# A two-layer decoder trunk on one core: an earlier pivot for the norms, squares folded group by group, and the tokens that the last layer doesn't need

## The reference

```python
def _layer_norm(x, g, b):
    mu = jnp.mean(xf, axis=-1, keepdims=True)
    var = jnp.mean(jnp.square(xf - mu), axis=-1, keepdims=True)
    y = (xf - mu) * lax.rsqrt(var + LN_EPS) * g.astype(jnp.float32) + b.astype(jnp.float32)
...
    for l in range(DEPTH):
        m = _mixer(h, ...)
        h = _layer_norm(ALPHA * h + m, ln1_g[l], ln1_b[l])
        f = _conv_ffn(h, w_up[l], conv_w[l], conv_b[l], w_down[l])
        h = _layer_norm(ALPHA * h + f, ln2_g[l], ln2_b[l])
    return h[:, N_META:, :]
```

## Time and profile before

| | before |
|---|---|
| median of 3 runs | 2676.42 us (2675.54 to 2681.03) |
| the profiled execution | 2678.43 us |
| its span, first to last instruction | 2676.6 us |
| mean granted TensorE clock | 0.974 |
| TensorE matmul busy | 2549.4 us, 95% |
| VectorE busy | 1775.6 us, 66% |
| ScalarE busy | 1368.8 us, 51% |

### The profile page before, as it was taken

The page is one execution under the profiler, slowest core; times in us unless marked ns, Lnnn a source line. Parts: engine busy times, 40 slices in busy tenths (PEclk is TensorE's granted clock), DMA queues, the critical chain, the costliest instruction groups (busy, mean ns, idle before and its releaser), DMA issues.

```text
span 2676.6 us, 55946 instructions
## 1 busy us (share of the span) xinstructions
PE 2549.4 (95%) x21738; PEld 2464.7 (92%) x21738; DVE 1775.6 (66%) x2782; ACT 1368.8 (51%) x2127; POOL 11.9 (0%) x19
## 2 busy tenths in 40 slices
PE   6999999889999999999979999998899999999997
PEld 5999788879999999999979997888899999999997
DVE  6887487676666666544488874877766666664445
ACT  5444365365555555433364444653666666553334
POOL 0000000000000000000000000000000000000000
PEclk7999999989999999999989999998899999999998
DMA  4433133345555555555444331333455555555553
GB/s 170 143 121 125 66 109 103 126 134 177 169 179 174 170 179 171 177 173 165 166 144 146 120 129 60 113 101 118 149 181 180 180 188 181 179 183 189 173 187 107
DMA packets 109733, 401.91 MB, mean 150 GB/s; under 512 B 12177, under 2 KB 12177, under 8 KB 109585
## 3 DMA queue, kind: packets, MB, share of 16 engines
q1 hardware_dynamic: 108432, 395.15, 44.9%
q0 software_dynamic: 1152, 4.63, 0.4%
HBM read 397.50 MB, written 2.23 MB: 149 GB/s over the span
## 4 chain that ended last, share of the span: by engine, by line
PE 89%; DVE 7%; ACT 2%; issue 1%; DMA 1%; SPq 0%; ACTq 0%; DVEq 0%
PE ps L426 22%; PE ps L427 22%; PE ps L428 22%; PE ps L525 4%; PE ps L527 4%; PE ps L526 4%; PE ps L675 3%; PE ps L491 1%; PE ps L662 1%; PE ps L641 1%; PE ps L608 1%; DVE h L1183 1%; PE ps L500 1%; PE ps L505 1%; DVE h L1162 1%
## 5 line engine op out<-in xcount | busy, mean ns | idle before, releaser
L786 ACT ACTIVATE w_hi<-raw 128x1024 fp32r<-128x1024 f32 x728 | 763.3, 1056 | 765.4 <-PE ps L428 656.7
L1107 DVE TENSOR_TENSOR w_lo<-raw,w_hi 128x1024 fp32r<-128x1024 f32 x528 | 638.9, 1224 | 543.9 <-ACT w_hi L786 543.8
L427 PE MATMUL ps<-x_lo,w_hi 128*128 128x272 f32 (+1 forms) x2944 | 841.3, 286 | 0.0
L428 PE MATMUL ps<-x_hi,w_hi 128*128 128x272 f32 (+1 forms) x2944 | 839.9, 285 | 0.0
L426 PE MATMUL ps<-x_hi,w_lo 128*128 128x272 f32 (+1 forms) x2816 | 805.5, 286 | 18.8 <-DVE x_lo L1191 18.4
L428 PEld LDWEIGHTS ps<-x_hi,w_hi 128*128 128x128 f32 x2944 | 555.5, 189 | 0.0
L427 PEld LDWEIGHTS ps<-x_lo,w_hi 128*128 128x128 f32 x2944 | 555.4, 189 | 0.0
L426 PEld LDWEIGHTS ps<-x_hi,w_lo 128*128 128x128 f32 x2816 | 531.2, 189 | 20.5 <-issue 18.0
L426 PE MATMUL ps<-g_hi,w_lo 128*128 128x272 f32 (+1 forms) x1408 | 403.7, 287 | 4.9 <-DVE w_lo L1107 2.5
L427 PE MATMUL ps<-g_lo,w_hi 128*128 128x272 f32 (+1 forms) x1408 | 403.0, 286 | 0.0
L428 PE MATMUL ps<-g_hi,w_hi 128*128 128x272 f32 (+1 forms) x1408 | 401.4, 285 | 0.0
(11 more groups left out here) (266 smaller groups left out, 3306.1 us busy)
## 6 DMA issues: line engine op xcount, KB each, us to landing
raw<-stream SPq DMA_DIRECT2D x744, 512.0 KB, 3.4
h<-x SPq DMA_DIRECT2D x4, 544.0 KB, 6.3
out<-h SPq DMA_DIRECT2D x4, 544.0 KB, 2.7
cst<-consts POOLq DMA_DIRECT2D x2, 724.0 KB, 6.5
wkv<-w_kv POOLq DMA_DIRECT2D x2, 512.0 KB, 7.9
b_st<-ssm_b POOLq DMA_DIRECT2D x2, 512.0 KB, 9.3
c_st<-ssm_c POOLq DMA_DIRECT2D x2, 512.0 KB, 11.3
par<-params SPq DMA_DIRECT2D x1, 562.0 KB, 12.1
```

The source lines that it names most:

```text
L427: pe.matmul(acc, w_hi[:, slot, kk, cols], lo, start=False, stop=False)
L428: mm = pe.matmul(acc, w_hi[:, slot, kk, cols], hi, start=False, stop=k == tiles - 1)
L786: act.activation(w_hi[:, slot, :, :], raw[:, slot, :, :], ACT.Copy).then_inc(hi_made, 1)
L1107: dve.tensor_tensor(w_low(phase, slot), raw[:, slot, :, :], w_hi[:, slot, :, :].bitcast(F32), ALU.subtract).then_inc(in_lo_made if phase = ...
```

## The change

The pivot is the mean of the first four tiles (two groups) instead of twelve: `sum_pivot` adds them, one matmul of ones follows group 2, and `take_pivot` copies it, scaled, into a tile of its own. `center_early` adds the pivot to the first six tiles in one instruction. From group 3 on the pivot is added to h before the group's product arrives (`before_out`, `before_down`), and the product on top. Each group is squared by ScalarE as it ends (`group_square`), folded by VectorE (`fold_squares`, now in five parts) and added into hsum (`sum_means`), so that TensorE sums hsum and the last group for the mean. In down, input times alpha is prepared in the phase (`before_down`), and `after_down` is one add.

In `layer_norm` on VectorE the first shift of four tiles moves behind the spread. After out, the first low part of up moves ahead of the residual of the last group, and three instead of two low parts lie in the scaling loop; after down one stays ahead of the shift, and again three instead of two lie in the loop. The order of scaling, x_lo and shifts in the loop changes.

On TensorE, out and down have bodies of eight groups and are no longer loops. g_hi and g_lo become halves of one tensor, and down of the last layer uses `wide_block`: w_hi with both in one matmul of 512 columns, w_lo with g_hi in one of 256; `after_down` adds both halves (two instructions). In the last layer the query tiles of the input projection (iq and fq, 12 of 30), late, gated, fox and out work on tokens 14 on; GpSimd zeroes the first 14 tokens of those tiles with two memsets, for which TensorE waits ahead of the S5 steps, and the residual of gated scales the first 14 columns with an instruction of its own.

```diff
 PHASES = {"in": (15, DT // KB, 1), "glu": (4, UT // KB, 4), "late": (2, DT // KB, 2), "gated": (8, UT // KB, 4),
-          "fox": (8, 1, 1), "out": (8, 1, 4), "up": (FT, DT // KB, 2), "down": (8, FT // KB, 4)}
+          "fox": (8, 1, 1), "out": (8, 1, 8), "up": (FT, DT // KB, 2), "down": (8, FT // KB, 8)}
...
-PIVOT = 3 * DT // 4
+PIVOT = 4
+EARLY = 6
...
+        def group_done(n, g):
+            return first_group((n - 1) // 2, "out" if n % 2 else "down") + g + 3
...
-                with pe.Fori(0, groups // body) as it:
+                with ExitStack() as loop:
+                    it = loop.enter_context(pe.Fori(0, groups // body)) if groups > body else 0
...
+            def wide_block(phase, slot, b, bank, tiles, both, ready, t0):
+                lo_w, n = w_low(phase, slot), NT - t0
+                for kk in range(KB):
+                    k = b * KB + kk
+                    if ready and k % 2 == 0:
+                        pe.wait_ge(*ready(k))
+                    hi_lo = both(k)[:, :, t0:NT]
+                    for j in range(2):
+                        cols = slice(j * P, j * P + P)
+                        pe.matmul(ps[:, bank + j, 0:2 * n].rearrange("p (h t) -> p h t", h=2), w_hi[:, slot, kk, cols], hi_lo,
+                                  start=k == 0, stop=False)
+                        mm = pe.matmul(ps[:, bank + j, 0:n], lo_w[:, kk, cols], hi_lo[:, 0, :], start=False, stop=k == tiles - 1)
+                mm.then_inc(block_used, 1)
...
-                for g in range(PIVOT // 2, 8):
-                    pe.wait_ge(centered, norm_base(n) + 4 + g - PIVOT // 2)
-                    for k in range(2 * g, 2 * g + 2):
-                        mm = pe.matmul(ps[:, 5, 0:NT], ones[:, :], h[:, k, :], start=k == PIVOT, stop=k == DT - 1)
+                last = [(h, DT - 2), (h, DT - 1)]
+                folded = [(hsum, 0), (hsum, 1)]
+                for i, (part, k) in enumerate(last + folded if n % 2 else folded + last):
+                    if k == DT - 2:
+                        pe.wait_ge(psum_free, group_done(n, 7))
+                    elif k == 0:
+                        pe.wait_ge(mean_summed, n)
+                    mm = pe.matmul(ps[:, 5, 0:NT], ones[:, :], part[:, k, :], start=i == 0, stop=i == 3)
                 mm.then_inc(mean_made, 1)
-                pe.wait_ge(sq_summed, n + 1)
-                for k in range(4):
-                    if k == 2:
-                        pe.wait_ge(squared, norm_base(n) + 5)
-                    tile = squares_of(n)[:, k if k < 2 else DT - 4 + k, :]
-                    mm = pe.matmul(ps[:, 6, 0:NT], ones[:, :], tile, start=k == 0, stop=k == 3)
+                for i, k in enumerate((DT - 2, DT - 1, 0, 1)):
+                    if k == DT - 2:
+                        pe.wait_ge(squared, squared_by(n, NORM_PARTS - 1))
+                    elif k == 0:
+                        pe.wait_ge(sq_summed, n + 1)
+                    mm = pe.matmul(ps[:, 6, 0:NT], ones[:, :], squares_of(n)[:, k, :], start=i == 0, stop=i == 3)
                 mm.then_inc(var_made, 1)
...
-                    acc = ps[:, t if t < WIDE else t % 2, 0:NT]
+                    t0 = query_t0(l) if IQ0 <= t < IQ0 + 8 or FQ0 <= t < FQ0 + 4 else 0
+                    acc = ps[:, t if t < WIDE else t % 2, t0:NT]
...
                     cast(l, "up", n)
+                    if n < 3:
+                        group_square(ln, 4 + n)
...
+                    if n == 3 * blocks + 10:
+                        early_square(ln + 1)
+                    if n >= 4 * blocks and n % blocks == 6:
+                        group_square(ln + 1, n // blocks - 1)
...
+                dve.tensor_tensor(h[:, 0:EARLY, :], h[:, 0:EARLY, :], spread(pivot[:, :], EARLY), ALU.add).then_inc(centered, 1)
...
-                    unshifted = [unshift(0)]
                     dve.wait_ge(var_made, n + 1)
                     after()
                     dve.scalar_tensor_tensor(out=rstd[:, :], in0=ps[:, 6, 0:NT], scalar=1.0 / D_MODEL, in1=shift_sq,
                                              op0=ALU.mult, op1=ALU.subtract).then_inc(spread_made, 1)
-                    if low_parts:
-                        low_part(*low_parts, 1)
+                    unshifted = [unshift(0)]
                 else:
...
-                late_lows = (1, 4, 5, 6) if n == 0 else (3, 5) if low_parts and low_parts[1] == "up" else (4, 6)
+                late_lows = (1, 4, 5, 6) if n == 0 else (2, 4, 6) if n % 2 else (4, 6, 7)
...
-                    if n and c in (0, 2, 4):
+                    if (c == 1 or c >= 3) and n < 2 * DEPTH:
+                        part = max(c - 2, 0)
+                        dve.wait_ge(xhi_made, CHUNKS * n + part + 1)
+                        t = slice(2 * part, 2 * part + 2)
+                        dve.tensor_tensor(x_lo[:, t, :], h[:, t, :], x_hi[:, t, :].bitcast(F32),
+                                          ALU.subtract).then_inc(xlo_made, 1)
+                    if n and c in (1, 3, 5):
                         unshifted.append(unshift(c // 2 + 1))
                     if low_parts and c in late_lows:
                         low_part(*low_parts, 4 - len(late_lows) + late_lows.index(c))
-                    if c >= 2 and n < 2 * DEPTH:
-                        dve.wait_ge(xhi_made, CHUNKS * n + c - 1)
-                        t = slice(2 * c - 4, 2 * c - 2)
-                        dve.tensor_tensor(x_lo[:, t, :], h[:, t, :], x_hi[:, t, :].bitcast(F32),
-                                          ALU.subtract).then_inc(xlo_made, 1)
...
+            def before_out(l, g):
+                h2 = h[:, 2 * g:2 * g + 2, :]
+                dve.wait_ge(psum_free, first_group(l, "fox") + g + 3)
+                after()
+                sums["before"] = mark(dve.tensor_tensor(h2, h2, spread(pivot[:, :], 2), ALU.add))
+            def before_down(l, g):
+                h2, hi, lo = (x[:, 2 * g:2 * g + 2, :] for x in (h, x_hi, x_lo))
+                dve.wait_ge(block_used, first_block(l, "down") + 1)
+                mark(dve.scalar_tensor_tensor(out=h2, in0=hi.bitcast(F32), scalar=1.0, in1=lo.bitcast(F32), op0=ALU.mult, op1=ALU.add))
+                after()
+                if g < 3:
+                    mark(dve.tensor_scalar(h2, h2, ALPHA, None, ALU.mult))
+                else:
+                    mark(dve.scalar_tensor_tensor(out=h2, in0=h2, scalar=ALPHA, in1=spread(pivot[:, :], 2), op0=ALU.mult, op1=ALU.add))
+            def after_down(l, g):
+                bank = 2 * (g % 2)
+                dve.wait_ge(block_used, first_block(l, "down") + PHASES["down"][1] * (g + 1))
+                h2, t0 = h[:, 2 * g:2 * g + 2, :], LAST_T0[1] if l == DEPTH - 1 else 0
+                n = NT - t0
+                after()
+                if t0:
+                    mark(dve.tensor_tensor(h2[:, :, t0:NT], h2[:, :, t0:NT], ps[:, bank:bank + 2, 0:n], ALU.add))
                     after()
-                    n = PIVOT // 2 * (2 * l + (phase == "down")) + g
-                    if g == 2:
-                        dve.wait_ge(pivot_made, 2 * (2 * l + (phase == "down")) + 1)
-                    if g == 0:
-                        dve.tensor_copy(hsum[:, :, :], h2).then_inc(h_summed, 1)
-                    else:
-                        dve.wait_ge(h_summed, n)
-                        dve.tensor_tensor(hsum[:, :, :], hsum[:, :, :], h2, ALU.add).then_inc(h_summed, 1)
+                    dve.tensor_tensor(h2[:, :, t0:NT], h2[:, :, t0:NT], ps[:, bank:bank + 2, n:2 * n], ALU.add).then_inc(psum_free, 1)
+                else:
+                    dve.tensor_tensor(h2, h2, ps[:, bank:bank + 2, 0:NT], ALU.add).then_inc(psum_free, 1)
...
-                for g in range(7):
+                for g in range(8):
                     if g < 5:
                         low_part(l, "out", g + 3)
+                    if g == 7:
+                        low_part(l, "up", 0)
                     residual(l, "out", g)
-                for c in range(4):
-                    take_pivot(ln, c)
-                for c in range(1, 4):
-                    fold_squares(ln, c)
-                residual(l, "out", 7)
+                    if g < 2:
+                        sum_pivot(ln, g)
+                    if g == 2:
+                        take_pivot(ln)
+                    if g == 3:
+                        center_early(ln)
+                    if g >= 4:
+                        sum_means(ln, g - 1)
+                    if g == 5:
+                        fold_squares(ln, 0)
+                    if 2 <= g < 7:
+                        before_out(l, g + 1)
+                    if g == 6:
+                        fold_squares(ln, 1)
+                for part in range(2, 5):
+                    fold_squares(ln, part)
                 layer_norm(ln, (l, "up"))
...
-                        if g == 7 and n < 8:
-                            take_pivot(ln + 1, n - 4)
-                        if g == 7 and 8 <= n < 11:
```

(18 more changed lines are left out.)

147 lines of the change are left out of this document (96 added, 51 removed).

## The result

| | before | after |
|---|---|---|
| median | 2676.07 us (2675.54 to 2681.03, 4 runs) | 2651.38 us (2649.61 to 2653.91, 4 runs) |
| ratio after / before | | 0.9904, 95% interval 0.9892 to 0.9916 |
| span of the profiled execution | 2676.6 us | 2647.8 us |

What follows compares the result with a forecast made beforehand. TensorE, busy for 95% of the span, was taken as the bound: two long matmul streams with short interruptions. Five terms, 3.7 + 7.9 + 8.5 + 7.2 + 6.2 = 33.5 us, gave a median of 2642.9 us, range 2633 to 2656.

Steps and rivals of the forecast that it cites:

- rival 1: Last down: a wide matmul costs as much as two narrow ones, giving 2651.4 us; chance 0.12.
- A: Out and down, both layers: one pivot sum per phase instead of two, four of eight go, saving 3.7 us.
- B: Out and down written out: down's stop at the loop's return and the slow clock behind it go, saving 7.9 us.
- Rival 2: Down: TensorE's stops come with the stretch of code, not the loop's return, giving 2650.8 us; chance 0.10.
- C: Last layer's down: two 256-column matmuls become one of 512 in 704 places, 12 ns saved each, 8.5 us.
- rival 3: Last down: the wide matmul hides more, saving near the upper bound of 14 us, giving 2637.4 us; chance 0.13.
- D: Last layer's queries: 1536 matmuls of 258 instead of 272 columns, saving 7.2 us, bounds 4 and 8.3.
- nine tenths: Last layer's narrower query matmuls: share of the remaining saving counted, after 0.5 us lost in fox, giving 7.2 us.
- E: Norms after out and down: earlier sums less a longer loop, saving 6.2 us in all, bounds 1 and 9.5.
- rival 4: Norms return everything: the last residual of out is delayed or TensorE waits for banks, 2649.1 us; chance 0.12.
- Rival 5: Last down: the two-part moving operand slows the wide matmul, making the kernel slower than before, 3130 us; chance 0.03.

Runs made afterwards that it cites:

- n4: The kernel before with everything of the change except the new norms: 2661.36 us, ratio 0.9932 to before.
- n3: The kernel before with out and down written out on TensorE instead of looped, both pivot sums kept: 2668.41 us against 2679.25, ratio 0.9963.
- n8: The kernel before, loops kept, with down leaving out its w_hi x lo product in 4 of 11 blocks: 2612.59 us in a single run, against 2676.43.
- n9: The kernel before with up on TensorE as 11 turns of four groups instead of 22 of two: 2676.01 us in a single run, beside 2680.98.
- n2: The changed kernel with all 272 columns again for the queries of the last layer: 2658.89 us, ratio 0.9925 to before.
- n5: The changed kernel run once more, unaltered, on another chip: 2653.80 us against 2676.43 for before, ratio 0.9910.
- n6: The changed kernel with VectorE's next shift (in the first norm the low part) ahead of the first x_lo: 2645.54 us, ratio 0.9885 to before.

## Why the prediction was right or wrong, point by point

- **Bound, and the sign.** Right: TensorE's stream and its interruptions set the time, and nothing new became the bound. 2651.38 lies in the range, 8.5 us above the forecast, at rival 1's number, though rival 1 is not what happened.
- **A, one pivot instead of two.** Forecast 0.93 us each. Shown: 0.91 (n4 against n3), 3.6 us in all.
- **B, written-out loops.** Forecast 7.9. Shown: 9.3 by stages, 9.9 (6.4 to 13.7) timed. The mechanism is right; the size was low because in layer 0 the second turn lost more than the stop and its slow stretch (5.1 us instead of 4.0; in layer 1 4.2 instead of 3.95). What it lost there beyond them is open. The slow stretch, 2.7 us of the term, is not bound to the stop: n8 and n9 stop and keep a clock of 1.00. Rival 2 (stops stay) fell: in after TensorE waits for nothing in either down. The reason given there, 2112 instructions against 2048, was too simple, since 1910 stop too. The Trainium skill says in Runtime: NRT & Kernel Launch, section Instruction fetch mechanics, that TensorE holds 2048 instructions, refilled in blocks of 256, and that a taken branch outside a window of two blocks must fetch. The packets of 16 KB, one for about 250 instructions, agree with the blocks. Turns of 800 and 1460 that return without a fetch speak against a window of two blocks. That a turn must also leave room for blocks cut at both ends and one read ahead fits 1460 and 1910, but it is only argued.
- **C, wide matmuls.** Forecast 8.5, shown 3.8. The failed step is "each matmul pays its columns plus about 12 ns". The rows had 256, 258 and 272 columns, a span of 16, and were read by counting the matmuls of a window. That count takes in those that overlap its ends, and the window of 256 columns also held a pivot sum of 0.93 us. Read from start to start, the same stretches give 118.3, 120.0 and 125.3 ns instead of 118.7, 119.6 and 125.0. From 256 to 272 that is 0.44 ns a column and some 6 ns for the matmul, from 258 to 272 it is 0.38 and 22, so the rows alone did not settle it. From 256 to 512 columns the price is 0.443 ns a column and 5 ns for the matmul, so merging two saves one share of 5 to 6 ns. The lower bound (0) held it, and rival 3, which would carry the small slope on, was wrong in its sign: the slope is steeper than the clock, not flatter. The formula that the prediction took from the Trainium skill (TensorE: Matmul & The Clock Gate, section Back-to-back issue gap), columns / 2.4 + 2.5 ns, is given there for a single matmul by itself, 216 ns for 512 columns, and the section has about 131 ns for such a matmul in a stream with weight loads. The 231.6 ns measured here agree with neither.
- **D, fewer columns.** Forecast 7.2, shown about 4.6 by stages (4 to 6 timed), within the bounds of 4 and 8.3. In the projection 2.1 us instead of 3.1: from the first S5 matmul on TensorE waits 3.6 us in n2 and 4.0 in n5, which explains 0.4 of the missing 1.0 (in the profiled execution of after these waits are only 2.5, and the stretch as long as in n5); the rest is open. From the squares of the gate to the last product of out 2.5 of about 4.1: TensorE's waits grew from 8.3 us in n2 to 9.6 in after, and the rest is open too. The nine tenths were too high (as written, they give 7.3 in all, not 7.2); the rows had said that TensorE waits there for 11.5 of 240 us, and the prediction charged one wait only.
- **E, the norms.** After out: sums 3.5 us earlier (3.6 forecast), 1.2 on the sums (1.7), loop 2.4 longer (2.5), so 2.3 instead of 2.8 (layer 1: 3.4 in the lucky execution, 1.9 in n5). The sums began 3.07 us after the last product, just outside the 2 to 3 promised, and the second group of up 31.7 us after them (32 promised). After down 0.3 (0.2), at the end 0.8 (0.4). TensorE waits for no bank in out: rival 4's margin held. The early centering took 1.85 us, the value that was taken, though the line as stated gives 1.68. What failed is what was not looked at: the first norm uses the same loop, and loses 1.3 us. E is 2 x 2.3 + 1.1 - 1.3 = 4.4, not 6.2. The 2.4 us of the longer loop were taken as the price of a low part; half of it was the idle VectorE that n6 removes.
- **Sum.** 3.6 + 9.3 + 3.8 + 4.6 + 4.4 = 25.7 us, against 24.1 and 24.7 measured. Three terms (C, D and E) were too high by 4.7, 2.6 and 1.8, one (B) too low by 1.4. The upper bounds of the terms add up to 44.1 us, not 43.4, which moves the lower end of the range by 0.7 and changes nothing here.
- **Rival 5** (slower by the wide operand) fell: 231.6 ns where it decides from 273.

## What to carry to other kernels

When code that moves is shared (a norm's loop), read the trace of each of its calls, the first one too, and look in it for the engine that now arrives too early: an instruction moved ahead of its data turns cover into a wait, and putting independent work before it brought 5.2 us more, by stages, in a kernel that had just gained 24. A cost per instruction and a cost per column can't be told apart from rows that differ by 6% in size when each is good to 0.3 or 0.4 ns; read paces from start to start, without other instructions in the window, and measure one far point before you merge instructions. Keep the body of a loop on TensorE near the 1460 instructions that returned freely here or below, or write it out, and look for the packets of the instruction queue at each return.

## What the runs showed of the hardware

- TensorE refetches a loop's body of 1910 instructions or more at the return (2.4 to 2.8 us from the last matmul's start to the next; in before 3.4 us of slow clock behind it, in n8 and n9 none); bodies of 400, 800 and 1460 return without a stop and with no block fetched.
- A matmul stream costs 118.3, 125.3, 175.3 and 231.6 ns for 256, 272, 384 and 512 columns at 2.4 GHz; one piece or two makes no difference.
- Behind an idle time of 3.4 us the same program ran once at 1.00 and once at 0.71 mean clock over the next 4 us. Between executions of one program such stretches differed by some 6 us in all (115.4 and 121.1 us at 1.2 GHz), and the times by 4 to 5 us. Differences of 0.1% need the stages, not the medians.
